# A two-layer mixer decoder step: Delta head steps and the gate chain in other slots, rounded products of a unit pair ahead of the low ones

## What is computed

```python
def _layer(x, pos, st, lp):
    h = _rmsnorm(x, lp['norm_mix_pre'])
    y, new_st = _token_mixers(h, pos, st, lp)
    x = x + _rmsnorm(y, lp['norm_mix_post'])
    h = _rmsnorm(x, lp['norm_mlp_pre'])
    u = jnp.square(jax.nn.relu(jnp.einsum('btd,df->btf', h, lp['w_up'])))
    x = x + _rmsnorm(jnp.einsum('btf,fd->btd', u, lp['w_down']), lp['norm_mlp_post'])
    return x, new_st
```

```python
ig = GATE_SOFTCAP * jnp.tanh((ia + gate_b[:H_A]) / GATE_SOFTCAP)
lf = jax.nn.log_sigmoid(GATE_SOFTCAP * jnp.tanh((fa + gate_b[H_A:]) / GATE_SOFTCAP))
g = -jnp.exp(lp['gdn_A_log'].astype(f32)) * jax.nn.softplus(ac + lp['gdn_dt_bias'].astype(f32))
beta = jax.nn.sigmoid(bcz)
```

## Time and profile before

| | us |
|---|---|
| median of 3 runs (3130.93 to 3133.9) | 3132.81 |
| the profiled execution | 3133.82 |
| its span, first to last instruction | 3132.2 |
| PE busy | 3049.4 |
| DVE busy | 1923.8 |
| ACT busy | 1543.6 |

### The profile page before, as it was taken

How to read it: one execution, slowest core, us unless ns; L and a number is a source line. 1 busy time by engine, 2 the same in 40 slices (tenths; PEclk the granted TensorE clock), 3 DMA queues, 4 the chain that set the end, 5 groups by cost and what they waited for, 6 DMA issues and landing times.

```text
span 3132.2 us, 66919 instructions
## 1 busy us (share of the span) xinstructions
PE 3049.4 (97%) x22980; PEld 2980.1 (95%) x22980; DVE 1923.8 (61%) x4002; ACT 1543.6 (49%) x3580; POOL 85.2 (3%) x163
## 2 busy tenths in 40 slices
PE   8999999999999999999999999999999999999998
PEld 7999999998999999999979999999989999999997
DVE  6677786656545545455576777766565455554555
ACT  5476665545433334334455676655454333343343
POOL 1100000000000000000001000000000000000000
PEclk9999999999999999999999999999999999999999
DMA  6554445553544444445445444454544445444444
GB/s 205 176 154 143 140 144 161 165 183 128 169 161 161 168 163 165 161 163 167 155 133 183 149 147 143 140 166 159 167 135 162 163 163 170 161 165 165 164 163 155
DMA packets 267111, 499.89 MB, mean 160 GB/s; under 512 B 34512, under 2 KB 39792, under 8 KB 266928
## 3 DMA queue, kind: packets, MB, share of 16 engines
q1 hardware_dynamic: 244080, 443.58, 43.9%
q0 software_dynamic: 14784, 51.05, 4.6%
q10 hardware_dynamic: 8064, 2.80, 0.3%
HBM read 475.32 MB, written 22.01 MB: 159 GB/s over the span
## 4 chain that ended last, share of the span: by engine, by line
PE 79%; DVE 12%; ACT 5%; issue 3%; DMA 2%; ACTq 0%; SPq 0%; DVEq 0%; POOL 0%; POOLq 0%
PE PU L522 71%; DVE WL L1293 3%; PE PE_ L522 2%; PE PABCD L522 2%; PE PF L522 2%; DMA RAW<-in_w 2%; ACT AE L892 1%; ACT Y L892 1%; DVE AE L1683 1%; ACT WH L892 1%; DVE Y L1477 1%; DVE Y L1313 1%; DVE X L1320 0%; DVE HL L1298 0%; DVE AM L1592 0%
## 5 line engine op out<-in xcount | busy, mean ns | idle before, releaser
L522 PE MATMUL PU<-HH,WH 128*128 128x288 f32 x4000 | 1235.4, 309 | 32.5 <-DVE HL L1298 21.0
L892 ACT ACTIVATE WH<-RAW 128x512 fp32r<-128x512 f32 x1669 | 965.9, 621 | 586.6 <-PE PU L522 431.9
L1293 DVE TENSOR_TENSOR WL<-RAW,WH 128x512 fp32r<-128x512 f32 x1668 | 1077.0, 687 | 277.6 <-ACT WH L892 261.5
L522 PE MATMUL PU<-HL,WH 128*128 128x288 f32 x4000 | 1183.3, 296 | 0.0
L522 PE MATMUL PU<-HH,WL 128*128 128x288 f32 x4000 | 1180.2, 295 | 0.0
L522 PEld LDWEIGHTS PU<-HH,WH 128*128 128x128 f32 x4000 | 754.7, 189 | 64.5 <-issue 45.3
L522 PE MATMUL PU<-UH,WH 128*128 128x288 f32 x2560 | 759.1, 297 | 2.8 <-DVE UL L1468 1.9
L522 PEld LDWEIGHTS PU<-HL,WH 128*128 128x128 f32 x4000 | 756.1, 189 | 3.6
L522 PEld LDWEIGHTS PU<-HH,WL 128*128 128x128 f32 x4000 | 756.0, 189 | 0.0
L522 PE MATMUL PU<-UL,WH 128*128 128x288 f32 x2560 | 755.2, 295 | 0.0
L522 PE MATMUL PU<-UH,WL 128*128 128x288 f32 x2560 | 752.6, 294 | 0.0
(11 more groups left out here) (279 smaller groups left out, 2204.7 us busy)
## 6 DMA issues: line engine op xcount, KB each, us to landing
RAW<-in_w SPq DMA_DIRECT2D x1669, 256.0 KB, 3.7
SIN<-in_sin POOLq DMA_DIRECT2D x32, 512.0 KB, 4.9
out_sout<-Y POOLq DMA_DIRECT2D x32, 512.0 KB, 5.4
BC<-gate_rows POOLq DMA_DIRECT2D x32, 304.0 KB, 4.6
AUX<-in_aux POOLq DMA_DIRECT2D x32, 152.0 KB, 3.9
X<-in_x SPq DMA_DIRECT2D x4, 576.0 KB, 8.7
out_y<-X SPq DMA_DIRECT2D x8, 288.0 KB, 2.1
out_sout<-SOUT ACTq DMA_DIRECT2D x32, 64.0 KB, 2.4
```

Source lines behind the costliest of these rows:

```text
L522: return nc.tensor.matmul(out, lhsT, rhs, start=start, stop=stop, skip_group_check=True)
L892: return nc.scalar.activation(out, in_, f, **kw)
L1293: tt(WL[s % 2][:, k], RAW[c][:], WH[s % 2][:, k].bitcast(F32), ALU.subtract).then_inc(sem("lo_ready"), 1)
```

## The change

1. **Pair order.** `pair_part` replaces the side-by-side order. Even slots hold for two chunks the products of HH with WH and WL of both units (8 matmuls), odd slots those of HL with WH (4).
2. **Weight roundings a pair ahead** at the three block ends: piece 4 of the next quad is rounded by ACT and DVE before the norm's scale, and pieces 5 to 7 take the places of 4 to 6. The weighing of the last chunk of Y (`weigh`) goes behind the scale.
3. **Gate chain.** Sum and reciprocal on DVE at slot 21 instead of 24 (one sum over all rows in place of two); capped, beta, y and abs go from DVE to ACT, slot 24; later steps move to slots 28 and 29 and to slots 1, 3, 7 and 10 of the next quad. The first head's rotation moves from slots 19 to 22 to slots 20, 23, 25 and 26.
4. **Delta heads.** `gdn_store` goes from slot 4 to 7 ("Delta copy"), `sample_state` from slot 27 to 28, behind the unit's matmuls and ahead of `head_sums`, `add_state` from slot 29 to slot 30, behind `finish_log`.
5. **Start.** ACT issues the load of `NG0` itself and waits for it behind its first weight piece; POOL issues the gate weights only when the second part of X has landed.

```diff
-ROTATE_SLOTS, FIRST_ROTATE_SLOTS = (16, 17, 19, 21), (19, 20, 21, 22)
+ROTATE_SLOTS, FIRST_ROTATE_SLOTS = (16, 17, 19, 21), (20, 23, 25, 26)
...
-            pool.dma_start(NG0[:], d["ng0"][0]).then_inc(sem("first_gain_in"), 16)
+            held("x_in1", 16)
             load_gate_weights(0)
...
+            def pair_part(Q, t, kind, l):
+
+                kk, low = divmod(t, 2)
+                e = 2 * l + (1 if kind == "up_first" else 0)
+                if t == 0:
+                    pe.wait_ge(sem("psum_read"), 4 * Q + 2)
+                if not low and kk % 2 == 0:
+                    pe.wait_ge(sem("lo_ready"), 16 * Q + 4 + kk // 2 + 1)
+                for s in range(2):
+                    psum = PU[s][:, 0:T]
+                    for k in (2 * kk, 2 * kk + 1):
+                        if s == 0:
+                            pe.wait_ge(sem("hl_ready" if low else "hh_ready"), e * NC_ + k + 1)
+                        if low:
+                            last = mm(psum, WH[s][:, k], HL[:, k], False, k == NC_ - 1)
+                        else:
+                            mm(psum, WH[s][:, k], HH[:, k], k == 0, False)
+                            mm(psum, WL[s][:, k], HH[:, k], False, False)
+                    if t == 15:
+                        last.then_inc(sem("unit_done"), 1)
...
                 if t == 28:
+
+                    pe.wait_ge(sem("state_kept"), n + 1)
+                    sample_state(n)
                     pe.wait_ge(sem("gdn_head"), nk + 1)
                     head_sums(n)
-                if t == 27:
-
-                    pe.wait_ge(sem("state_kept"), n + 1)
-                    sample_state(n)
...
+            act.dma_start(NG0[:], d["ng0"][0]).then_inc(sem("gain_at_start_in"), 16)
...
-                    if (e or l) and g in (0, 1, 3, 5):
-                        hi_part(Q, (g + 1) // 2 + 4)
+                    if (e or l) and g in (0, 2, 4):
+                        hi_part(Q, g // 2 + 5)
...
-                if k == -1 and t == 25:
+                if k == -1 and t == 24:
+
+                    act.wait_ge(*gate("rec", l))
+                    fn(GU[0:64], GE[0:64], scale=-2.0 * SOFTCAP, bias=SOFTCAP).then_inc(gate("capped", 0)[0], 1)
+                    fn(ROWA[96:128], GE[96:128]).then_inc(gate("beta", 0)[0], 1)
+                    fn(ZG[0:64], GE[0:64], scale=2.0 * SOFTCAP, bias=-SOFTCAP).then_inc(gate("y", 0)[0], 1)
+
+                    act.wait_ge(*gate("y", l))
+                    fn(GE, ZG, ACT.Abs).then_inc(gate("abs", 0)[0], 1)
                     act.wait_ge(*gate("abs", l))
...
             def after_out(l):
+                Q = l * QUADS + HEADS + NC_ // 4
+                hi_part(Q, 4)
                 norm_scale(2 * l + 1, RS, "rs_ready")
-                prenorm(l, 2, NG[:, 1], l * QUADS + HEADS + NC_ // 4)
+                weigh(l, 0, NC_ - 1)
+                prenorm(l, 2, NG[:, 1], Q)
...
-                if t == 29:
-                    add_state(n)
                 if t == 30:
                     finish_log(n)
+                    add_state(n)
...
-                    if done and t == 4:
+                    if done and t == 7:
                         gdn_store(l, done)
...
             def update_and_split(l, which, lo_l, lo_which, lo_gain, Q):
 
+                lo_part(Q, 4)
                 for g in range(8):
...
                     if g in (1, 3, 5):
-                        lo_part(Q, g // 2 + 4)
+                        lo_part(Q, g // 2 + 5)
                 prenorm_lo(lo_l, lo_which, lo_gain, range(14, 16))
-                lo_part(Q, 7)
```

More of the change, by code:

```diff
@@ L82 @@
 LAST_SLOTS = {0: 0, 1: 1, 2: 3, 3: 6, 10: 8, 4: 9, 5: 9, 8: 11}
-SIDE_BY_SIDE = [(t % 2, t // 2) for t in range(16)] + [divmod(t, 8) for t in range(16, SLOTS)]
 JOINED = [(0, kk) for kk in range(7)] + [(1, kk) for kk in range(7)] + [(0, 7), (1, 7)] + [divmod(t, 8) for t in range(16, SLOTS)]
@@ L525, in turn @@
                 return nc.tensor.transpose(out, in_, IDENT)
+            def pair_part(Q, t, kind, l):
[17 more added lines that the diff above has]
+                        last.then_inc(sem("unit_done"), 1)
             def unit_part(Q, t, kind, l, x, joined):
-                s, kk = JOINED[t] if joined else SIDE_BY_SIDE[t] if two_at_once(kind, l) else divmod(t, 8)
+                if two_at_once(kind, l) and t < 16:
+                    pair_part(Q, t, kind, l)
+                    return
+                s, kk = JOINED[t] if joined else divmod(t, 8)
                 hi, lo = (UH, UL) if kind in ("out", "down", "down0", "down_last") else (HH, HL)
@@ L909, in prenorm @@
             def prenorm(l, e, gain, Q):
-                if e == 0:
-                    act.wait_ge(sem("first_gain_in"), 16 * (l + 1))
-                else:
+                if e:
                     act.wait_ge(sem("gains_in"), 16 * (l + 1))
+                elif l:
+                    act.wait_ge(sem("first_gain_in"), 16 * l)
                 which = e // 2
@@ L965, in output_squares, with weigh @@
                     act.wait_ge(sem("gains_in"), 16 * (l + 1))
-                gain = NG[:, 0 if kind == "out" else 2, c:c + 1]
-                fn(Y[:, c], Y[:, c], scale=gain).then_inc(sem("output_squares"), 1)
+                if c < NC_ - 1:
+                    weigh(l, 0 if kind == "out" else 2, c)
+            def weigh(l, which, c):
+                fn(Y[:, c], Y[:, c], scale=NG[:, which, c:c + 1]).then_inc(sem("output_squares"), 1)
             def norm_scale(count, dst, name):
@@ L1364, in gates @@
                     stt(CSUM, GT, -1.0, GE, ALU.add, ALU.subtract).then_inc(gate("rest", 0)[0], 1)
-                if k == -1 and t == 28:
+                if k == 0 and t == 1:
                     dve.wait_ge(*gate("log", l))
@@ L1373, in gates @@
                     ts(GT, GT, GP[:, 1:2], -1.0, ALU.mult, ALU.mult).then_inc(gate("decay", 0)[0], 1)
-                if k == -1 and t == 29:
+                if k == 0 and t == 3:
                     ts(EXTI[:, 1:EXT_P], GU[0:H_A, 0:SEQ], 1.0, None, ALU.mult).then_inc(gate("ext", 0)[0], 1)
@@ L1393, in gates @@
                     nc.vector.tensor_tensor_scan(EXTM, EXTF, EXTI, 0.0, ALU.add, ALU.max).then_inc(gate("scan", 0)[0], 1)
-                if k == 0 and t == 6:
+                if k == 0 and t == 7:
                     em = EXTM[:, EXT_P:EXT].rearrange("p (b t) -> p b t", b=NB)
```

37 lines of the change are left out of this document (16 added, 21 removed).

## The result

The changed kernel takes 3113.92 us in the median of four runs (3112.79 to 3114.77), the kernel before 3133.36 on the same chip (3130.93 to 3136.43). The ratio is 0.9937, with a 95% interval of 0.9921 to 0.9953: 19.4 us faster, where 11.7 us were forecast. The time lies in the range (3111 to 3131), 7 us under the predicted 3121. The profiled execution's span went from 3132.2 to 3113.2 us, so one trace of each shows nearly the same 19.0 us.

The account below looks back on a forecast made before the run. PE, busy 3049.4 of 3132.2 us, was taken as the bound, leaving about 83 idle us and half-clock stretches to win. 1.2 + 4.6 + 4.6 + 2.2 + 3.1 - 4 = 11.7 us saved; median 3121, range 3111 to 3131.

Parts of the forecast that it names:

- Start: Kernel start: ACT's first weight rounding at about 6.3 us and no wait for the second piece; 1.2 us saved.
- Gate chain, layer 0: Layer 0's gate chain: 3.1 us of PE waits and 1.5 of half clock go; 4.6 us saved, bounds 2 and 5.5.
- Gate chain, layer 1: The same gate chain waits in layer 1, 4.2 us before; 4.6 us saved, bounds 2.5 and 5.5.
- up_first: Block ends before up_first: low weights ready sooner, ACT's next rounding 1.1 us sooner; 2 x 1.1 = 2.2 us saved.
- the pair order does nothing: Rival at the block ends: only ACT's start after unit 0 counts; 3123, within the forecast's range, no separate chance given.
- sample_state: Delta heads: sample_state one slot later takes away PE's waits for SOUT in 14 heads; 3.1 us saved.
- The Delta copy: Delta heads, gdn_store to slot 7: the wait moves from slot 7 to 9, nothing saved; bounds -0.1 and +0.5 us a head.
- AUX: Delta heads: later add_state delays store and AUX load; five of 12 heads lose 0.85 us each, 4 us lost.
- the forecast's own sign: Slot 8 of Delta heads: ACT not idle for AUX, or idle over 1 us in most heads, means the Delta part is wrong.
- the store fits: Rival, Delta heads: AUX still lands in time and the Delta copy saves something; 3113 to 3117, chance 0.20.
- Weights behind the store: Rival, Delta heads: weight loads beside the later store come late, up to 1 us in 14 heads; 3131, chance 0.13.
- slower: Rival, Delta heads: late store and AUX cost about 1.9 us in each of 12 heads; 3140, chance 0.06.

Follow-up runs that it names:

- the controls: The changed kernel itself run twice more with nothing changed; ratios to the kernel before 0.9938 and 0.9939.
- the experiment: Changed kernel with one part put back: gate chain in old slots (gate stretches 25.4 and 22.0 us against 19.3 and 19.1), or sample_state at slot 27 (Delta stretches 2.2 us more).
- the dose: Changed kernel with POOL issuing BC ahead of AUX, so that AUX lands later; Delta heads took 21.9 us more than in the changed kernel.
- d_add29: Changed kernel with only add_state back at slot 29, ahead of finish_log; ratio to the kernel before 0.9946.
- d_copy4: Changed kernel with only the Delta copy (gdn_store) back at slot 4; whole kernel 0.28% (8.8 us) more, Delta heads 7.0 us more.
- d_auxsecond: Changed kernel with POOL issuing BC ahead of AUX, the same run as the dose; Delta heads took 21.9 us more than in the changed kernel.
- b_copy7: Kernel before with only the Delta copy (gdn_store) moved from slot 4 to 7; 6.1 us less in the median, Delta heads 6.7 us less.

## Why the prediction came out as it did

- **Start.** 1.2 forecast, 1.0 measured (0.8 in the controls). ACT starts at 6.52 us, not 6.3, since its data landed that much later. The step held, as far as the timeline shows; no run has this edit alone.
- **Gate chain, layer 0.** 4.6 forecast, 5.6 measured, 6.1 by the experiment. All waits are gone, the 0.4 us for the spread of k too, and the clock stayed full. The mechanism held; the clock's part and the last wait were sized low, and the whole lies a little above the stated bound of 5.5.
- **Gate chain, layer 1.** 4.6 forecast, 3.4 measured (3.1 and 3.4 in the controls), 2.9 by the experiment. With the stretch ahead taken in it is 3.8 (3.4 and 3.9), and 4.1 by the experiment. The forecast took layer 1 to be like layer 0. It isn't: the wait for the spread of k stayed with 1.4 us, not 0.4, since ACT's roundings ahead of it wait for weight pieces; the timeline of ACT there shows it.

```profile
1598.55 0.63 ACT L913 ACTIVATE WH<-RAW 128x512 fp32r<-128x512 f32 x1 [1.36 <-DMA RAW<-in_w]
```

- **up_first.** 2 x 1.1 forecast, 2 x 0.7 measured. The step that waits of 1 us and more go from the pair's end, and that one of about 1.3 us stands before PE_, held to a tenth (1.31). ACT's rounding was forecast at 748.5 - 745.49 = 3.0 us behind the last pair of HH; it came 3.25 behind it. That the order itself costs 0.9 us against the roundings alone was not seen: the forecast weighed the two edits only together, and its rival ("the pair order does nothing") asked the question too kindly. It does harm.
- **sample_state.** 3.1 forecast; 3.6 measured in the part of the heads where it stands (14 x 0.26), and 3.6 again by the experiment. Held, a little low.
- **The Delta copy.** Nothing forecast, 6.7 to 7.0 us measured. This is the step that failed. It took what is left at slot 7 from the first Delta head (0.27 us in the earlier trace rows), as if the copy were all that sets that head apart. It isn't. In the first head of the changed kernel slot 7's first matmul is at 188.95 us and DVE's sum (L1635) starts at 189.75, 0.80 later; in the heads behind it this is 0.20 in eleven and 0.3 in three, and in the eleven DVE even waits for PE. DVE is behind there from further ahead: its step at L1625 starts 2.06 us before that matmul in the first head and 2.5 to 2.9 in the others. So the rest at slot 7 is nothing, save in the two first heads (0.6 us in 2 waits above). At slot 9 the forecast had 0.35, measured are 0.10 to 0.25. Together 0.62 forecast and 0.1 to 0.25 measured, and the difference, 0.4 us in each of 14 heads, is what the forecast lacks. Its upper bound (+0.5 a head) was the truth.
- **AUX.** 4 us lost forecast, about 2 measured (the heads with CB at 5.77 and 6.25). The chain up to ACT was right: AUX lands after ACT wants it in all 12 heads, later even than forecast (2.0 us of idling in the mean), since with the wait at slot 7 gone ACT is there sooner. The chain behind ACT was wrong. I had DVE's rounding of slot 9 behind ACT's rounding of the same slot, but DVE is one piece behind ACT. By the dose ACT may start CB up to 4.9 us behind slot 7's first matmul at no cost; it is ready for it at about 2.8 (the 4.76 of the head above, less its idle time of 2.02). That is 2.2 us of cover, where the forecast had 0.55. An AUX in time would not start CB at 2.8, though: in d_add29 ACT then stands idle for DVE's Z and starts CB at 3.18 in most heads, so what AUX can be late by at no cost is about 1.7 us. And by the forecast's own sign (ACT idle for AUX in most heads for over 1 us) this part was to be called wrong, as it is.
- **The rivals.** The time is in the band of "the store fits" (3113 to 3117), yet not for its reason, since AUX is late in every head. "Weights behind the store" did not occur at the size that this rival needs. The piece issued beside the store of 343.40 us landed after 3.8 us (DMA issues from 343.30 to 343.45 us: size, us to landing). The 14 such pieces of the changed kernel's Delta heads took 3.5 to 4.6 us, 3.9 in the median (4.2 and 4.1 in the controls), those of the kernel before 3.4 to 3.7, 3.5 in the median, and PE has no wait for WL in these heads.

```profile
out_sout<-Y POOLq DMA_DIRECT2D x1, 512.0 KB, 5.2
RAW<-in_w SPq DMA_DIRECT2D x1, 256.0 KB, 3.8
```

  The Trainium skill (DMA: Bandwidth & Descriptors, on queues, rings and completion order) has a DMA engine go round its queues packet by packet, from which this rival made a piece at a third of the engines. These landings show it slowed by 0.4 to 0.7 us in the median against the kernel before; what limits either transfer here was not measured. The "slower" rival needed AUX to be late by more than its cover in every head; two of 12 were. (The last 0.2 in its sum of 1.9 us a head has no row behind it.)

Right in sign and inside its range, then, but 7.7 us short: the sum of 11.7 has two errors of one direction, both in the Delta heads, where 1 us was to be lost and 7.7 were gained. A rest at slots 7 and 9 was taken from a head that is not like the others (6.7 to 7.0 us), and a cover was taken too short (about 2 us). The other terms missed by 1.2 us or less each, in both directions, and nearly cancel; that they do is luck.

## What to carry to other kernels

A copy or store of the previous step that stands ahead of a result that the bounding engine waits for should go behind it; what it then costs is read from the steady heads, not from the first one. Whether a late transfer costs time is decided by the first instruction behind it that shares an engine with the critical chain, so follow each wait to the semaphore count it needs: an engine that runs one piece behind another has a whole piece more of cover. And of two edits that come together (an order and its data ahead of time), each is worth a run by itself: here one brought the gain and the other took part of it.

## What the runs showed of the hardware

- A wait of PE costs more than its length once the clock falls. In the Delta heads of these kernels the granted clock stayed at 1.00 behind waits of up to 1.00 us (d_copy4) and fell behind the four of 1.05 to 1.71 us (d_auxsecond), and what followed took 1.6 to 3.0 us longer than the 31.29 of the other heads, beside some 1.2 to 1.7 us right behind the longer three. But at the end of up_first, 1.86 and 1.97 us in the kernel before had 1.00 behind them, and 1.97 us in b_copy7 had 0.63 and 0.67 in the 4 us behind it, so the length of the wait alone doesn't decide it.
- Landing times of the same transfer in the same program vary: AUX (152 KB) between 2.4 and 5.8 us in the heads of the changed kernel (7.9 once at the start of layer 1), weight pieces (256 KB) up to 6.5 us in one Delta head of d_add29 where the median of all is 3.7. Late AUX shows in two heads of 12 in the changed kernel. Three executions of its code differ by 1.9 us in the Delta heads and by 1.5 in the retention heads, and their spans by 3 us (3113.2, 3114.4, 3116.2).
